# Prompt's recurrence: the next chunk's k clamped two levels sooner, its b less log k before the decayed k, ACT's exponential of b one chunk ahead

## What is computed

```python
def step(S, inp):                       # one chunk of tokens, all heads
    qc, kc, vc, gc = inp
    b = jnp.cumsum(gc, axis=2)          # gc = log f, k = 1 - f
    inter = jnp.einsum('bhtd,bhdv->bhtv', qc * jnp.exp(b), S)
    diff = b[:, :, :, None, :] - b[:, :, None, :, :]
    decay = jnp.exp(jnp.where(mask[:, :, None], diff, -jnp.inf))
    A = jnp.einsum('bhtd,bhtsd,bhsd->bhts', qc, decay, kc)
    o = inter + jnp.einsum('bhts,bhsv->bhtv', A, vc)
    bl = b[:, :, -1:, :]
    S = jnp.exp(bl[:, :, 0])[..., None] * S + jnp.einsum('bhsd,bhsv->bhdv', kc * jnp.exp(bl - b), vc)
    return S, o
```

## Time and profile before

| what | value |
|---|---|
| time, median of 3 runs | 4665.18 us (4661.82 to 4665.87) |
| the profiled execution's own time | 4667.56 us |
| span of the profile | 4666.0 us |
| busy share of the span: PE, PEld, DVE, ACT, POOL | 86%, 68%, 59%, 43%, 8% |
| recurrence of the prompt | about 756 to 1046 us of the span |

### The profile page before, as it was taken

The page is one execution under the profiler, slowest core; times in us unless marked ns, Lnnn a source line. Parts: engine busy times, 40 slices in busy tenths (PEclk is TensorE's granted clock), DMA queues, the critical chain, the costliest instruction groups (busy, mean ns, idle before and its releaser), DMA issues. The chain is left out here.

```text
span 4666.0 us, 53789 instructions
## 1 busy us (share of the span) xinstructions
PE 3997.4 (86%) x19288; PEld 3154.5 (68%) x19289; DVE 2771.1 (59%) x4753; ACT 1996.3 (43%) x3151; POOL 370.5 (8%) x379
## 2 busy tenths in 40 slices
PE   8999997768777588853799977999999999999998
PEld 7888876654455244442688866787878787877884
DVE  5678655883488798887588835434534453454320
ACT  3333324552378599873677732233223213322310
POOL 0000002444210011100100000000000000000000
PEclk9999977889678799875899988999999999999967
DMA  5555553324210244331311023323423342334345
GB/s 159 159 172 156 147 145 99 91 80 116 70 27 23 65 165 150 136 103 59 88 45 33 14 100 109 90 92 104 135 83 99 100 135 82 94 98 128 95 138 184
DMA packets 481968, 486.30 MB, mean 104 GB/s; under 512 B 96152, under 2 KB 396152, under 8 KB 473144
## 3 DMA queue, kind: packets, MB, share of 16 engines
q1 hardware_dynamic: 457336, 364.53, 26.9%
q0 software_dynamic: 23104, 118.50, 7.2%
q10 hardware_dynamic: 1280, 0.02, 0.0%
HBM read 422.07 MB, written 60.90 MB: 104 GB/s over the span
## 5 line engine op out<-in xcount | busy, mean ns | idle before, releaser
L2578 ACT ACTIVATE weight_parts<-weights 128x1024 fp32r<-128x1024 f32 x296 | 313.4, 1060 | 1193.0 <-PE acc L2905 560.0
L2905 PE MATMUL acc<-act_T,weight_parts 128*128 128x512 f32 x3072 | 705.7, 392 | 18.1 <-DVE act_T L2700 18.1
L2929 PE MATMUL acc<-weight_parts,hidden_parts 128*128 128x512 f32 x3072 | 702.2, 391 | 9.3 <-DVE product_rows L2707 9.3
L2693 DVE TENSOR_TENSOR weight_parts<-weights,weight_parts 128x1024 fp32r<-128x1024 f32 x296 | 362.9, 1227 | 570.7 <-ACT weight_parts L2578 570.7
L2905 PEld LDWEIGHTS acc<-act_T,weight_parts 128*128 128x128 f32 x3072 | 582.4, 190 | 140.7 <-issue 12.2
L2929 PEld LDWEIGHTS acc<-weight_parts,hidden_parts 128*128 128x128 f32 x3072 | 580.0, 189 | 131.6 <-issue 6.1
L533 PE MATMUL accumulated<-hT,w_in_parts 128*128 128x512 f32 (+1 forms) x1920 | 430.4, 390 | 4.4 <-DVE w_in_parts L386 4.4
L533 PEld LDWEIGHTS accumulated<-hT,w_in_parts 128*128 128x128 f32 x1920 | 367.1, 215 | 66.0 <-DVE w_in_parts L386 6.4
L2788 DVE TENSOR_SCALAR hidden_T<-acc 128x512 f32<-128x512 f32 (+1 forms) x160 | 95.7, 598 | 445.3 <-PE acc L2905 356.0
L307 ACT ACTIVATE w_in_parts<-w_in_raw 128x1024 fp32r<-128x1024 f32 (+1 forms) x140 | 141.9, 1015 | 461.7 <-PE accumulated L533 264.6
L2346 DVE TENSOR_SCALAR_CACHE_REDUCE junk_dve<-score,candidate 128x2048 bf16<-128x2048 f32 (+6 forms) x224 | 321.6, 1467 | 9.7 <-DVE candidate L2322 8.2
(11 more groups left out here) (366 smaller groups left out, 6494.2 us busy)
## 6 DMA issues: line engine op xcount, KB each, us to landing
weights<-in_w_up SPq DMA_DIRECT2D x160, 512.0 KB, 4.0
weights<-in_w_down SPq DMA_DIRECT2D x160, 512.0 KB, 3.6
w_in_raw<-in_w_in SPq DMA_DIRECT2D x100, 512.0 KB, 3.9
weights<-in_w_out SPq DMA_DIRECT2D x40, 512.0 KB, 3.6
w_in_raw<-in_w_in SPq DMA_DIRECT2D x60, 256.0 KB, 3.3
x_sb<-in_x_prompt POOLq DMA_DIRECT2D x4, 2048.0 KB, 9.8
q_rows<-scratch_qT SPq DMA_DIRECT2D x64, 128.0 KB, 3.5
mix_in<-scratch_mix POOLq DMA_DIRECT2D x4, 2048.0 KB, 9.4
```

What stands on the lines that cost most here:

```text
L2578: act.activation(w2[:, w, 0, :], raw[:, b[0], :], ACT.Copy).then_inc(hi_rdy, 1)
L2693: dve.tensor_tensor(w2[:, w, 1, :], raw[:, b, :], w2[:, w, 0, :].bitcast(F32), ALU.subtract).then_inc(lo_rdy, 1)
L2905: mm = pe.matmul(acc[:, u % 8, 0:w], w2[:, u % 2, b, k * P:(k + 1) * P], aT[:, a, k, 0:w], start=(k == 0 and (a, b) == (0, 0)), stop=(k == ...
L2929: mm = pe.matmul(acc[0:pt, 2 * t + half, :], hs[:, d % 2, a, t * pt:(t + 1) * pt], w2[:, d % 2, b, half * ST:(half + 1) * ST], start=(d == ...
```

## The change

The same instructions run, with the same operands and sizes, in other places. On VectorE clamp_k of the next chunk stands after the level n = 3 (behind the state's update) and not after n = 5, and less_log_k of the next chunk stands after n = 6, ahead of the multiply of k_decayed and not behind it. On ScalarE exp_b of the next chunk stands at the end of a chunk, ahead of the wait for the turned k, and not at the start of the next. exp_b of the first chunk is made before the loop.

```diff
-                def body(g, j, par):
-                    first = isinstance(g, int) and g == 0
+                def exp_b(g, j, par):
                     act.wait_ge(in_rdy[par], 64 * j + 64)
                     if not (isinstance(g, int) and g < 2):
                         act.wait_ge(s_rdy, g - 1)
                     act.activation(eb[:, par, :, :], bt[:, par, :, :], ACT.Exp).then_inc(eb_done, 1)
+
+                def body(g, j, par):
+                    first = isinstance(g, int) and g == 0
                     act.wait_ge(bk_rdy, g + 1)
...
                     if not first:
                         act.wait_ge(s_done, g)
                         roots(g - 1)
+                    if not is_last(g):
+                        exp_b(g + 1, j + par, 1 - par)
                     act.wait_ge(kdT_done, g + 1)
                     act.activation(kdn[:, :, :].rearrange("p h t -> p (h t)"), pT[:, :], ACT.Copy).then_inc(kdn_rdy, 1)
                 log_k(0)
+                exp_b(0, 0, 0)
                 chunks(act, body)
...
-                        if n == 5 and not is_last(g):
+                        if n == 3 and not is_last(g):
                             clamp_k(g + 1, j + par, 1 - par)
+                        if n == 6 and not is_last(g):
+                            less_log_k(g + 1, 1 - par)
                     dve.wait_ge(decay_rdy, g + 1)
                     dve.tensor_tensor(kd[:, :, :], kd[:, :, :], kt[:, par, :, :], ALU.mult).then_inc(kd_rdy, 1)
-                    if not is_last(g):
-                        less_log_k(g + 1, 1 - par)
                     pick(SLOTS - 1)
```

## The result

The changed kernel takes 4679.57 us (median of 7 runs, 4677.07 to 4682.12), the kernel before 4665.18 in the same comparison: ratio 1.0033, 95% interval 1.0021 to 1.0044. It is 14.4 us slower, above the top of the forecast's range.

A forecast was written before the change was run, and what follows sets the result against it. VectorE, taking turns with GpSimd, was taken to bound the b_less_log_k stage. Terms of -0.22 us a chunk gave 1.7 us, plus 1.9 for TensorE's clock: 3.6 faster, median 4661.5 us, eight in ten between 4653 and 4669.

The forecast's parts named there:

- the one on the clamp: VectorE's clamp, moved forward, sometimes waits for the next chunk's last load, r_v: 0.15 us a chunk, bounds 0 and about 1.
- Over 0.4 us in most chunks: Sign of being wrong: idle time before minus_b_mid, released by r_v's DMA, over 0.4 us in most chunks.
- the sum: Per-chunk terms on VectorE, -0.49+0.06+0.06+0.15 = -0.22 us, giving 1.7 us, plus 1.9 for TensorE's clock: 3.6 us faster.
- The term on the clamp's work: VectorE's clamp instructions two levels sooner: same work, cost 0.06 us a chunk, bounds 0 and 0.42.
- 1.9 us as gain for the clock: TensorE's 1.2 GHz stretch slides through the chunks; at 17.1 us a chunk the slide all but ends, saving 1.9 us.
- exp_b falls into ScalarE's wait: On ScalarE, exp_b's 0.53 us moves into the 1.65 us wait for the turned k_decayed and costs nothing.
- the level exponentials start where they did: On ScalarE, the level exponentials start 0.06 us later, within 0.1 us of their old place.
- GpSimd's gain ends in its own wait: GpSimd starts 0.59 us sooner but loses it at its third level, whose wait grows from 0.95 to 1.3-1.6 us.
- mix_rows comes under 0.2 us sooner: On VectorE, mix_rows was to begin 0.1 to 0.35 us sooner, taken as 0.25.
- The term for q_exp_b: On VectorE, q_exp_b catches its turn with GpSimd: 0.49 us sooner less 0.06, so 0.43, in eleven of thirteen full chunks.
- The rival "slower": The clamp waits for r_v in each chunk; at 1 us the kernel is 8 us slower, 4673 us; chance 0.14.
- The rival "the clock gives more": TensorE's slow stretch moves off the matmuls that pair_weights copies wait for: 4650 to 4658 us; chance 0.15.

The follow-up runs named there:

- e7: e1 with a bare VectorE wait for the next chunk's loads after n = 3, the clamp staying after n = 5: 4672.33 us, ratio 1.0016.
- w1: The changed kernel with TensorE making each chunk's q and k products three times, in its idle gap: 4671.48 us, ratio 1.0016.
- e8: The kernel before with only the clamp moved to after n = 3 and the next chunk's loads issued earlier: 4667.73 us, ratio 1.0007.
- e6: The kernel before with SyncE issuing the next chunk's loads earlier, ahead of the store and the gate's load: 4661.56 us, ratio 0.9992.
- e1: The changed kernel with the clamp put back after n = 5, the other moves kept: 4661.73 us, ratio 0.9996 to the kernel before.
- w2: The changed kernel with the next chunk's loads issued earlier and TensorE's q and k products made three times: 4653.37 us, ratio 0.9981.

## Why the prediction was wrong

The step that failed is the one on the clamp: "In some chunks it waits a few tenths, in some not. Bounds: 0 and about 1 us; I take 0.15 a chunk." The place was right (the loads of the next chunk, r_v last, and the cover down from 2.6 us to nothing), and so was its sign, but the size was not: 8.9 us are waited in nine chunks, 1.0 us each where it waits, 0.6 a chunk over the fourteen that have such a clamp and a load to come. Over 0.4 us in most chunks was one of the prediction's own signs of being wrong; it is so in eight of the fourteen. Measured by e7, the wait costs 10.6 us where the sum had 2. Two things were missed. The landing was reckoned from a median (4.3 us), while the clamp needs each chunk's own: from r_v's issue to the clamp that waited for it were 4.4 to 5.9 us in the nine chunks, and the median itself is now 4.7. Why it grew isn't shown. And the sum had the clamp and the last landing meet in every chunk (12.6 and 12.6), while the chunks are of two kinds. From 851.30 on there are five waits; one is the last clamp's, and the other four lie in chunks of one kind: q_exp_b has won its half microsecond there, so the clamp comes sooner, and SyncE issues r_v 8.95 us behind b_less_log_k and not 8.38. The gain between mix_rows and the clamp turned into waiting just there. w1 shows the same on a larger scale: a faster TensorE gave 8.1 us and not the 10.2 to 14.6 of the kernels that hardly wait.

The term on the clamp's work was mis-sized as well: "I take 0.06, near 0, as VectorE loses no work by it." In a chunk whose slow stretch lies where it always did that is right (17.38 in e8 against 17.30). But up to 6.2 us were lost by it in the stage. It puts the next level product 0.4 us later, TensorE idles longer for it (1.51 us in e8, 0.99 in e6), and some chunks have a second or a longer stretch at 1.2 GHz on the last levels, at 0.8 to 1.6 us each. That the longer idling brings these stretches is argued; the runs show both, and that most of the loss goes when another idle gap is filled. The prediction took 1.9 us as gain for the clock on the ground of a steady period. In e1, where nothing waits for the loads, no stretch is longer than 3.4 us any more. In the changed kernel the period was not steady (17.0 to 20.1 us in the full chunks), stretches of 6.8 us came back, and the mean granted clock stayed at 0.87.

What held: exp_b falls into ScalarE's wait; the level exponentials start where they did; GpSimd's gain ends in its own wait (1.42, forecast 1.3 to 1.6); mix_rows comes under 0.2 us sooner (forecast 0.1 to 0.35). The term for q_exp_b, 0.43 us in eleven chunks, held in half of them only, not "in nearly all". Its readiness of 0.35 us behind mix_rows was read off a chunk of the other kind; in the earlier trace rows q_exp_b starts 0.84 us behind it and takes 0.74, near the 0.69 it takes alone, so there it had lost no turn worth 0.49. In e1 the undisturbed chunks take 16.8 and 17.4 us in turn, against 17.30. Their mean is the 17.1 of the forecast, by luck: 0.5 us won in one half and 0.1 lost in the other. The net gain of these parts, e1, is 3.2 us in the medians, where the sum has about 6 for the same parts (11x0.43, less 0.3 for the other chunks, and the clock's 1.9); the interval of e1 includes no change.

The rival "slower" named this mechanism with 4673 us at 1 us a chunk, and slow-clock stretches with it, but its 4673 counts the wait alone (13x0.63) and nothing for the clock. With 0.6 a chunk of waiting the kernel was at 4679.6. The rival "the clock gives more" has a slip: its two terms, 8 and 8.9 us, make a least period of 16.9 us and not 16.7, and 4658 in place of 4655.5. As to the Trainium skill's figure, worked out as an estimate to 2.6 us for a load of this size (page "DMA: Bandwidth & Descriptors", section "Anatomy of one DMA"), it is for a transfer that GpSimd issues; here SyncE issued four in a row, and the trace has 4.7 for the last.

## What to carry to other kernels

Before an instruction moves forward in an engine's order, list every semaphore it waits for and find when each is reached in every chunk, not on the median: the one that was long reached at the old place, here a load with 2.6 us of slack (an estimate from a median), is the one that binds at the new place, and in an in-order queue all that stands behind pays. Then ask which other engine idles through that wait, and what its idling costs beyond the time itself. An addition of useless work in an idle gap (eight matmuls a chunk) was worth 0.2% of this kernel's time, and the reordering without its clamp nothing that could be told.

## What was not expected of the hardware

Waits of VectorE slowed TensorE's following matmuls as well: after 3.30 us without work the granted clock was 0.50 (1.2 GHz) over 6.82 us, and ten waits put into e1 (e7, 9.9 us in all) raised the time at 1.2 GHz from 38 to 55 us. In the kernel before such a stretch follows, in nearly each chunk, the idle gap of 2 us ahead of the first level product; when that gap was filled to 0.35 us no such stretch was left in 258 us, and the kernel was 11.2 us faster with 8 matmuls a chunk more. In w1 and w2 the same filling left some slow stretches; why these and not others is open.
